# The causal mask of a decay matrix: a minimum on VectorE in place of two TensorE matmuls, and additions moved ahead of a weight split

## The chip, the core and the metric

The kernel runs on one core of a Trainium2 chip. The metric is the device time of one execution in microseconds (us); lower is better. TensorE (PE in the profile) multiplies matrices, VectorE (DVE) and ScalarE (ACT) work elementwise, GpSimd (POOL) helps, and SyncE's queue (SPq) starts the loads. Each engine works through its own instructions in order; engines wait for each other on semaphores.

## What is computed

Two small models run one after the other, each of two layers on 256 tokens of width 1024. The change is in the first model, in its state space mixer ("SSD"), which works on two chunks of 128 tokens, 4 groups and 8 heads in a group:

```python
x = (xh * dt[..., None]).reshape(bsz, nc, SSD_CHUNK, SSD_GROUPS, SSD_HPG, p)
a_cum = jnp.cumsum(a_dt, axis=-1)
causal = jnp.tril(jnp.ones((SSD_CHUNK, SSD_CHUNK), dtype=bool))
decay = jnp.exp(jnp.where(causal, a_cum[..., :, None] - a_cum[..., None, :], -jnp.inf))
cb = jnp.einsum("bclgn,bcsgn->bgcls", cc, bc)
y_diag = jnp.einsum("bgecls,bcsgep->bclgep", cb[:, :, None] * decay, x)
```

`a_cum` only falls along the tokens, since every `dt * a` is negative. For each group, each chunk t and each of the 8 heads the kernel needs a 128 x 128 matrix exp(a_cum[l] - a_cum[s]) for l >= s and zero elsewhere.

## The kernel before

**Weights.** All weights stream from HBM in chunks of 128 x 2048 float32 (1 MB) through a ring of three slots. For precision each chunk is split: ScalarE writes a rounded copy (`split_high`, L964, tile `w_high`), VectorE writes the rest (`split_low`, L1325, tile `w_low`; every `tt` of VectorE is recorded at L1325), and TensorE makes three products of each pair (L524 to L526 for 512 columns, L752 to L754 for 256). ScalarE may split chunk c once TensorE is done with chunk c-3; SyncE may load chunk c+3 once VectorE has split chunk c.

**Slots.** Each engine's program of a layer is one loop over the chunks c, written out. In slot c ScalarE first runs `split_high(l, c)`, VectorE first `split_low(l, c)`, and behind it each runs whatever other work has that slot number; TensorE runs `before(l, c)`, the small matmuls of that slot, and then the products of chunk c. So everything that ScalarE or VectorE does in a slot stands between two splits.

**The SSD work of one group.** Group g starts with weight tile i = 2, 5, 8, 11 (`XT`), and its steps have slots counted from 2i:
- 2i+5: TensorE turns the convolved x of the group (`conv`) into banks 4 and 5. This *turn* waits for `ssd_y` of group g-1, since banks 4 and 5 still hold that group's result. For groups 1 to 3 slot 2i+5 is slot 2i'+11 of the group before (i' = i-3).
- 2i+6 and 2i+8: the *row spread* of chunk t = 0 and 1 (L606 and L608): for each of two banks one matmul of `ident_r` with `never_r` writes -1e30 where l < s and 0 elsewhere, and one matmul adds a_cum[l] of 4 heads, spread over all partitions, on top. GpSimd prepares its operand `decay_rows` (L1293).
- 2i+7 and 2i+9: ScalarE takes 8 exponentials of 128 x 128 from banks 6 and 7 into `ssd_decay` (EM in the code, L1083), with -a_cum[s] as bias; exp(-1e30) is zero.
- 2i+7: VectorE makes y = D x and xdt = dt x from banks 4 and 5 (four instructions). TensorE's state matmul (L614) into bank 6 waits for the exponentials of t = 0; ScalarE copies it out in slot 2i+8 (L1075), and the row spread of t = 1 waits for that copy.
- 2i+8 and 2i+10: VectorE multiplies `ssd_decay` by the masked C B product. TensorE multiplies by xdt in slots 2i+9 and 2i+10 (L633), and by the state in slot 2i+10 (L638).
- 2i+11 and 2i+12: VectorE adds the results into y: one instruction in the first slot, three in the second. The last one signals `ssd_y` for this group; GpSimd's gate (L1287, y times silu(z)) and the next turn wait for it.
- 2i+13: ScalarE squares the gated y (L1089), sums and takes the root; VectorE takes the reciprocal (L1482) and scales. It is the same slot as 2i+7 of the next group, and stands ahead of that group's y and xdt.
- 2i+15: VectorE weights the turned y (two instructions from PSUM), ScalarE rounds it (L1096), VectorE subtracts (two instructions into `b_low`). It is slot 2i+9 of the next group.
- Slots of other work between: a convolution on VectorE (slot 2i+10 for groups 0 to 2, 16 instructions, L1381 and L1384) and rotary embeddings (8 small instructions in slots 2i+7 of group 0 and 2i+9 of the others).

Of the kernel before, what the change touches and what calls it, by code (L numbers as in the profile page):

```python
# [17 lines left out]
F32R = mybir.dt.float32r  # L18
# [4 lines left out]
P = 128  # L23
# [113 lines left out]
def build(nc, stream1, stream2, pars, const1, const2, onehot, relb, final_g, ple_g, w_x, out, rev):  # L137
    ctx = ExitStack()
    with ctx:
# [23 lines left out]
        ident_r = sb("ident_r", [P, P], F32R)  # L163
        never_r = sb("never_r", [P, P], F32R)
# [150 lines left out]
        def signal(name, per):  # L315
            return Signal(sem(name), per)
# [55 lines left out]
        ssd_m = signal("ssd_m", 2 * GROUPS)  # L372
        ssd_y = signal("ssd_y", 2 * GROUPS)
# [148 lines left out]
        def _(pe):  # L522
# [19 lines left out]
            def before(l, c):  # L542
# [37 lines left out]
                for g, i in enumerate(XT):  # L580
                    if c == 2 * i + 5:
                        pe.wait_ge(conv_act.sem, conv_act.at(l, 3 + g))
                        if g == 0:
                            pe.wait_ge(btok_out.sem, btok_out.at(l, 1))
                            pe.wait_ge(cumt_out.sem, cumt_out.at(l, 1))
                        else:
                            pe.wait_ge(ssd_y.sem, ssd_y.at(l, 2 * g))
                        for t in range(T):
                            for j in range(4):
                                last = turn(ps[:, 4 + t, tok(j)], conv[:, j, tok(t)])  # L590
                        last.then_inc(xt_ps.sem, 1)
                    for t, at_c in ((0, 2 * i + 6), (1, 2 * i + 8)):
                        if c == at_c:

                            if t == 1:
                                pe.wait_ge(state_out.sem, state_out.at(l, g + 1))
                            elif g == 0:
                                pe.wait_ge(cb_masked.sem, cb_masked.at(l, 1))
                            else:
                                pe.wait_ge(ssd_y.sem, ssd_y.at(l, 2 * g))  # L600
                                pe.wait_ge(qk_out.sem, qk_out.at(l, g))

                            pe.wait_ge(decay_rows.sem, decay_rows.at(l, g + 1))
                            half_of = (tri_r, later_r)[t][:, P // 2 - 1:P // 2].to_broadcast([P, P])
                            for b in range(2):
                                nc.tensor.matmul(four(ps[:, 6 + b, :]), ident_r[:, :], bc(never_r[:, :].unsqueeze(1), 4, P),  # L606
                                                 start=True, stop=False)
                                last = nc.tensor.matmul(ps[:, 6 + b, :], half_of, DR[:, b * 512:(b + 1) * 512],  # L608
                                                        start=False, stop=True)
                            last.then_inc(row_ps.sem, 1)  # L610
                    if c == 2 * i + 7:
                        pe.wait_ge(xds_ready.sem, xds_ready.at(l, g + 1))
                        pe.wait_ge(ssd_exp.sem, ssd_exp.at(l, 2 * g + 1))
                        nc.tensor.matmul(ps[:, 6, :], btok[:, g, :], xds, start=True, stop=True).then_inc(state_ps.sem, 1)  # L614
# [11 lines left out]
                for g, i in enumerate(XT):  # L626
# [9 lines left out]
                    if c == 2 * i + 10:  # L636
                        pe.wait_ge(ssd_exp.sem, ssd_exp.at(l, 2 * g + 2))
# [315 lines left out]
        def _(act):  # L953
# [36 lines left out]
            with act.Fori(0, L) as l:  # L990
# [17 lines left out]
                for c in range(3, CHUNKS1):  # L1008
# [61 lines left out]
                    for g, i in enumerate(XT):  # L1070
# [5 lines left out]
                        for t, at_c in ((0, 2 * i + 7), (1, 2 * i + 9)):  # L1076
                            if c == at_c:
                                act.wait_ge(row_ps.sem, row_ps.at(l, 2 * g + t + 1))
                                if g:
                                    act.wait_ge(yd_ps.sem, yd_ps.at(l, 2 * (g - 1) + t + 1))  # L1080
                                for e in range(HPG):
                                    a = t * HEADS + g * HPG + e
                                    ins = nc.scalar.activation(EM[t][:, e, :], ps[:, 6 + e // 4, tok(e % 4)], ACT.Exp,  # L1083
# [182 lines left out]
        def _(pool):  # L1266
            pool.wait_ge(late_loaded, 16)
            nc.gpsimd.tensor_copy(ident_r[:, :], ident)
            nc.gpsimd.tensor_scalar(never_r[:, :], later, NEG, None, ALU.mult)
# [51 lines left out]
        def _(dve):  # L1321
# [76 lines left out]
            with dve.Fori(0, L) as l:  # L1398
# [37 lines left out]
                for c in range(3, CHUNKS1):  # L1436
                    split_low(l, c)
# [12 lines left out]
                    for g, i in enumerate(XT):  # L1450
# [5 lines left out]
                        if c == 2 * i + 7:  # L1456
# [8 lines left out]
                            ins.then_inc(xdt_ready.sem, 1)  # L1465
                        for t, at_c in ((0, 2 * i + 8), (1, 2 * i + 10)):
# [3 lines left out]
                        if c == 2 * i + 11:  # L1470
                            dve.wait_ge(yd_ps.sem, yd_ps.at(l, 2 * g + 1))
                            tt(y[:, 0, :], y[:, 0, :], ps[:, 4, :], ALU.add).then_inc(ssd_y.sem, 1)
                        if c == 2 * i + 12:
                            dve.wait_ge(yd_ps.sem, yd_ps.at(l, 2 * g + 2))
                            tt(y[:, 1, :], y[:, 1, :], ps[:, 5, :], ALU.add)
                            dve.wait_ge(off_ps.sem, off_ps.at(l, g + 1))
                            dve.wait_ge(decays.sem, decays.at(l, 1))
                            chain.then(dve, tt(heads(yoff), heads(ps[:, 7, :]), bc(dec_in[:, hs].unsqueeze(2), HPG, HD), ALU.mult))
                            tt(y[:, 1, :], y[:, 1, :], yoff, ALU.add).then_inc(ssd_y.sem, 1)
# [379 lines left out]
```

## Time and profile before

| | us |
|---|---|
| median of 3 runs | 1676.93 (1672.54 to 1677.43) |
| the profiled execution, its device time | 1677.54 |
| its span in the trace | 1675.6 |
| TensorE busy | 1584.4 (95%) |
| VectorE busy | 1022.4 (61%) |
| ScalarE busy | 844.9 (50%) |
| GpSimd busy | 64.3 (4%) |
| mean granted TensorE clock | 0.983 |

The span is that of one execution; 1.9 us of its device time lie around it. Matmuls overlap in the records, so the time that one costs is the distance between two starts, not its recorded duration. The steps of groups 1 and 2 repeat every 43.5 us (turns start at 126.59, 170.08 and 213.54 us), and the SSD work of the two layers lies at about 80 to 260 us and 723 to 903 us.

### The profile page before, as it was taken

The numbers are of one execution on the slowest core, as the hardware profiler recorded it, in microseconds if no ns is written. First come the engines' busy times: TensorE is split into PE (matmuls) and PEld (weight loads), VectorE is DVE, ScalarE is ACT, GpSimd is POOL, SyncE is SP. The second block draws the span as 40 slices with busy tenths as digits, with TensorE's granted clock in tenths as the row PEclk, the third lists the DMA queues.
The fourth block names the chain that finished last, engine by engine and source line by source line (L and its number), as shares of the span: only waits on it lengthen the run. The fifth ranks groups of instructions, "written<-read, shape, count | busy, mean of one in ns | idle before, by whom it ended". The sixth has DMA issues, their size and how long they took to land.

```text
span 1675.6 us, 21488 instructions
## 1 busy us (share of the span) xinstructions
PE 1584.4 (95%) x8006; PEld 1333.9 (80%) x8006; DVE 1022.4 (61%) x1287; ACT 844.9 (50%) x940; POOL 64.3 (4%) x38
## 2 busy tenths in 40 slices
PE   5999999999999997999999999999999799879987
PEld 4988888787778886988888788778888688668876
DVE  5977766545555444777775645565453665666664
ACT  3556666454354433556666444354443555554463
POOL 0001100000000000011100000000000010001000
PEclk9999999999999999999999999999999899999999
DMA  5443444444445553444444434345555453336250
GB/s 198 151 172 135 146 176 152 150 151 151 153 178 179 181 183 140 152 176 151 151 144 159 151 133 155 139 177 181 188 188 187 192 180 108 146 124 226 100 199 33
DMA packets 39666, 265.47 MB, mean 158 GB/s; under 512 B 4343, under 2 KB 5400, under 8 KB 9112
## 3 DMA queue, kind: packets, MB, share of 16 engines
q1 hardware_dynamic: 37800, 260.41, 43.4%
q10 hardware_dynamic: 1776, 3.83, 0.6%
q8 instruction: 60, 0.98, 0.2%
q14 instruction: 30, 0.25, 0.0%
HBM read 262.39 MB, written 1.84 MB: 158 GB/s over the span
## 4 chain that ended last, share of the span: by engine, by line
PE 83%; DVE 5%; issue 5%; ACT 5%; DMA 1%; ACTq 0%; DVEq 0%; SPq 0%
PE ps L524 22%; PE ps L526 21%; PE ps L525 21%; PE ps L529 4%; PE ps L752 3%; PE ps L753 3%; PE ps L754 3%; ACT w_high L964 2%; DVE scratch L1325 2%; PE ps L633 2%; ACT w_high L1154 1%; PE ps L667 1%; DVE w_low L1325 1%; DMA w_raw<-in_stream 1%; DVE h L1325 1%
## 5 line engine op out<-in xcount | busy, mean ns | idle before, releaser
L1325 DVE TENSOR_TENSOR w_low<-w_raw,w_high 128x2048 fp32r<-128x2048 f32 (+2 forms) x252 | 561.0, 2233 | 519.8 <-ACT w_high L964 441.0
L964 ACT ACTIVATE w_high<-w_raw 128x2048 fp32r<-128x2048 f32 (+1 forms) x198 | 372.6, 1884 | 426.4 <-PE ps L526 414.4
L524 PE MATMUL ps<-w_high,u_high 128*128 128x512 f32 x1376 | 553.2, 402 | 10.8 <-DVE w_low L1325 5.8
L526 PE MATMUL ps<-w_high,u_low 128*128 128x512 f32 x1376 | 541.1, 393 | 0.0
L525 PE MATMUL ps<-w_low,u_high 128*128 128x512 f32 x1376 | 540.4, 393 | 0.0
L524 PEld LDWEIGHTS ps<-w_high,u_high 128*128 128x128 f32 x1376 | 261.4, 190 | 67.7 <-issue 7.1
L526 PEld LDWEIGHTS ps<-w_high,u_low 128*128 128x128 f32 x1376 | 261.0, 190 | 56.2
L525 PEld LDWEIGHTS ps<-w_low,u_high 128*128 128x128 f32 x1376 | 261.5, 190 | 53.8 <-issue 1.9
L524 PE MATMUL ps<-w_high,b_high 128*128 128x512 f32 x384 | 151.7, 395 | 1.9 <-issue 1.9
L526 PE MATMUL ps<-w_high,b_low 128*128 128x512 f32 x384 | 149.7, 390 | 0.0
L525 PE MATMUL ps<-w_low,b_high 128*128 128x512 f32 x384 | 149.5, 389 | 0.0
L1154 ACT ACTIVATE w_high<-w_raw 128x2048 fp32r<-128x2048 f32 (+2 forms) x54 | 95.8, 1785 | 96.9 <-PE ps L526 85.2
L529 PE MATMUL ps<-con,scratch 128*128 128x128 f32 x592 | 86.8, 289 | 57.5 <-DVE scratch L1349 29.7
L529 PEld LDWEIGHTS ps<-con,scratch 128*128 128x128 f32 x592 | 73.7, 149 | 72.9 <-DVE scratch L1349 31.2
L752 PE MATMUL ps<-u_high,w_high 128*128 128x256 f32 x384 | 110.2, 287 | 0.0
L753 PE MATMUL ps<-u_low,w_high 128*128 128x256 f32 x384 | 108.7, 283 | 0.0
L754 PE MATMUL ps<-u_high,w_low 128*128 128x256 f32 x384 | 108.7, 283 | 0.0
L524 PEld LDWEIGHTS ps<-w_high,b_high 128*128 128x128 f32 x384 | 72.2, 188 | 16.7 <-issue 2.3
L526 PEld LDWEIGHTS ps<-w_high,b_low 128*128 128x128 f32 x384 | 72.1, 188 | 15.4
L525 PEld LDWEIGHTS ps<-w_low,b_high 128*128 128x128 f32 x384 | 72.2, 188 | 14.1
L752 PEld LDWEIGHTS ps<-u_high,w_high 128*128 128x128 f32 x384 | 73.8, 192 | 0.9 <-issue 0.5
L753 PEld LDWEIGHTS ps<-u_low,w_high 128*128 128x128 f32 x384 | 73.7, 192 | 0.8 <-issue 0.5
(224 smaller groups left out, 1400.9 us busy)
## 6 DMA issues: line engine op xcount, KB each, us to landing
w_raw<-in_stream SPq DMA_DIRECT2D x238, 1024.0 KB, 4.8
w_raw<-in_stream SPq DMA_DIRECT2D x10, 512.0 KB, 3.4
par<-in_pars SPq DMA_DIRECT2D x4, 265.0 KB, 5.0
h<-in_x SPq DMA_DIRECT2D x1, 1024.0 KB, 7.7
ple_gain<-in_ple_g ACTq DMA_DIRECT2D x2, 512.0 KB, 6.1
scratch<-rev ACTq DMA_DIRECT2D x2, 512.0 KB, 6.9
w_raw<-in_stream SPq DMA_DIRECT2D x4, 256.0 KB, 2.5
out<-h SPq DMA_DIRECT2D x2, 512.0 KB, 2.6
```

The source lines that it names most:

```text
L524: nc.tensor.matmul(o, hi, whi, start=start, stop=False, **kw)
L525: nc.tensor.matmul(o, hi, wlo, start=False, stop=False, **kw)
L526: return nc.tensor.matmul(o, lo, whi, start=False, stop=stop, **kw)
L529: return nc.tensor.transpose(o, i, ident)
L633: last = nc.tensor.matmul(ps[:, 4 + t, e * HD:(e + 1) * HD], EM[t][:, e, :], xdt[:, t, e * HD:(e + 1) * HD], start=True, stop=True)
L667: nc.tensor.matmul(ps[:, 4 + g // 2, (g % 2) * S:(g % 2 + 1) * S], qT[:, g, hh, tok(1)], kT[:, hh, :], start=True, stop=True)
L752: nc.tensor.matmul(o, WH[:, slot, w], uH[:, kk, :], start=first, stop=False, skip_group_check=True)
L753: nc.tensor.matmul(o, WH[:, slot, w], uL[:, kk, :], start=False, stop=False, skip_group_check=True)
L754: last = nc.tensor.matmul(o, WL[:, slot, w], uH[:, kk, :], start=False, stop=kk == KD - 1, skip_group_check=True)
L964: nc.scalar.activation(WH[:, c % RING, 0:n], W[:, c % RING, 0:n], ACT.Copy).then_inc(high_ready, 1)
L1154: nc.scalar.activation(WH[:, c % RING, 0:n], W[:, c % RING, 0:n], ACT.Copy).then_inc(high_ready, 1)
L1325: return nc.vector.tensor_tensor(out=o, in0=a, in1=b, op=op)
```

## The change

The two `never_r` matmuls of each row spread are gone, and the spread is a plain matmul. A new VectorE instruction in slots 2i+7 and 2i+9, behind y and xdt, takes min(a_cum[l], a_cum[s]) from banks 6 and 7 into `ssd_decay`; where l < s this is a_cum[s], so that the exponential is 1, and the product with the masked C B makes it zero. ScalarE's exponentials read and write `ssd_decay` in place. Who waited for the exponentials to free banks 6 and 7 now waits for the minimum (`row_clipped`). The additions into y keep their slot numbers but stand ahead of the slot's `split_low`.

```diff
                             for b in range(2):
-                                nc.tensor.matmul(four(ps[:, 6 + b, :]), ident_r[:, :], bc(never_r[:, :].unsqueeze(1), 4, P),
-                                                 start=True, stop=False)
                                 last = nc.tensor.matmul(ps[:, 6 + b, :], half_of, DR[:, b * 512:(b + 1) * 512],
-                                                        start=False, stop=True)
+                                                        start=True, stop=True)
                             last.then_inc(row_ps.sem, 1)
                     if c == 2 * i + 7:
                         pe.wait_ge(xds_ready.sem, xds_ready.at(l, g + 1))
-                        pe.wait_ge(ssd_exp.sem, ssd_exp.at(l, 2 * g + 1))
+                        pe.wait_ge(row_clipped.sem, row_clipped.at(l, 2 * g + 1))
...
                     if c == 2 * i + 10:
-                        pe.wait_ge(ssd_exp.sem, ssd_exp.at(l, 2 * g + 2))
+                        pe.wait_ge(row_clipped.sem, row_clipped.at(l, 2 * g + 2))
...
                             if c == at_c:
-                                act.wait_ge(row_ps.sem, row_ps.at(l, 2 * g + t + 1))
-                                if g:
-                                    act.wait_ge(yd_ps.sem, yd_ps.at(l, 2 * (g - 1) + t + 1))
+                                act.wait_ge(row_clipped.sem, row_clipped.at(l, 2 * g + t + 1))
                                 for e in range(HPG):
                                     a = t * HEADS + g * HPG + e
-                                    ins = nc.scalar.activation(EM[t][:, e, :], ps[:, 6 + e // 4, tok(e % 4)], ACT.Exp,
+                                    ins = nc.scalar.activation(EM[t][:, e, :], EM[t][:, e, :], ACT.Exp,
                                                                bias=nacum[:, a:a + 1])
...
             pool.wait_ge(late_loaded, 16)
-            nc.gpsimd.tensor_copy(ident_r[:, :], ident)
-            nc.gpsimd.tensor_scalar(never_r[:, :], later, NEG, None, ALU.mult)
...
                 for c in range(3, CHUNKS1):
+                    for g, i in enumerate(XT):
+                        if c == 2 * i + 11:
+                            dve.wait_ge(yd_ps.sem, yd_ps.at(l, 2 * g + 1))
+                            tt(Y[g % 2][:, 0, :], Y[g % 2][:, 0, :], ps[:, 4, :], ALU.add).then_inc(ssd_y.sem, 1)
+                        if c == 2 * i + 12:
+                            dve.wait_ge(yd_ps.sem, yd_ps.at(l, 2 * g + 2))
+                            tt(Y[g % 2][:, 1, :], Y[g % 2][:, 1, :], ps[:, 5, :], ALU.add)
...
+                            tt(Y[g % 2][:, 1, :], Y[g % 2][:, 1, :], yoff, ALU.add).then_inc(ssd_y.sem, 1)
                     split_low(l, c)
...
+                        for t, at_c in ((0, 2 * i + 7), (1, 2 * i + 9)):
+                            if c == at_c:
+                                dve.wait_ge(row_ps.sem, row_ps.at(l, 2 * g + t + 1))
+                                if g:
+                                    dve.wait_ge(yd_ps.sem, yd_ps.at(l, 2 * (g - 1) + t + 1))
+                                tt(EM[t], ps[:, 6:8, :].rearrange("p b (e l) -> p (b e) l", e=4),
+                                   bc(acum[:, t * HEADS + g * HPG:t * HEADS + (g + 1) * HPG].unsqueeze(2), HPG, P), ALU.min)\
+                                    .then_inc(row_clipped.sem, 1)
```

VectorE, before, from the end of slot 20 to the scaling in slot 23 (the additions of group 1 in slots 21 and 22; its `ssd_y` is the last `scratch<-scratch` row):

```order
L1384 SCALAR_TENSOR_TENSOR conv<-xpad,par,conv 128x256 x4
L1329 REGISTER_ALU
L1325 TENSOR_TENSOR w_low<-w_raw,w_high 128x2048
L1325 TENSOR_TENSOR scratch<-scratch,ps 128x512
L1329 REGISTER_ALU
L1325 TENSOR_TENSOR w_low<-w_raw,w_high 128x2048
L1325 TENSOR_TENSOR scratch<-scratch,ps 128x512
L1325 TENSOR_TENSOR scratch<-ps,small 128x512
L119 REGISTER_ALU
L1325 TENSOR_TENSOR scratch<-scratch 128x512
L1329 REGISTER_ALU
L1325 TENSOR_TENSOR w_low<-w_raw,w_high 128x2048
```

And the same place of the change, where the file's lines have shifted by 7 (`tt` is L1318):

```order
L1377 SCALAR_TENSOR_TENSOR conv<-xpad,par,conv 128x256 x4
L1318 TENSOR_TENSOR scratch<-scratch,ps 128x512
L1322 REGISTER_ALU
L1318 TENSOR_TENSOR w_low<-w_raw,w_high 128x2048
L1318 TENSOR_TENSOR scratch<-scratch,ps 128x512
L1318 TENSOR_TENSOR scratch<-ps,small 128x512
L119 REGISTER_ALU
L1318 TENSOR_TENSOR scratch<-scratch 128x512
L1322 REGISTER_ALU
L1318 TENSOR_TENSOR w_low<-w_raw,w_high 128x2048
L1322 REGISTER_ALU
L1318 TENSOR_TENSOR w_low<-w_raw,w_high 128x2048
```

One split fewer stands ahead of the last addition, and two splits in a row stand behind it.

VectorE, before, in slots 18 and 19 (the product of t = 0 of group 1, the weighting of group 0, its `b_low`, the rotary embedding):

```order
L1325 TENSOR_TENSOR w_low<-w_raw,w_high 128x2048
L1468 REGISTER_ALU
L1325 TENSOR_TENSOR ssd_decay_54<-ssd_decay_54,scratch 128x1024
L1329 REGISTER_ALU
L1325 TENSOR_TENSOR w_low<-w_raw,w_high 128x2048
L1325 TENSOR_TENSOR scratch<-ps,par 128x512 x2
L1325 TENSOR_TENSOR b_low<-scratch,b_high 128x4x128 x2
L1500 REGISTER_ALU
L1325 TENSOR_TENSOR scratch<-scratch,con 128x128
```

And of the change, from the last xdt instruction of slot 17 on:

```order
L1318 TENSOR_TENSOR xdt<-ps,small 128x512
L1473 REGISTER_ALU
L1318 TENSOR_TENSOR ssd_decay_54<-ps,small 128x1024
L1322 REGISTER_ALU
L1318 TENSOR_TENSOR w_low<-w_raw,w_high 128x2048
L1318 TENSOR_TENSOR ssd_decay_54<-ssd_decay_54,scratch 128x1024
L1322 REGISTER_ALU
L1318 TENSOR_TENSOR w_low<-w_raw,w_high 128x2048
L1318 TENSOR_TENSOR scratch<-ps,par 128x512 x2
L1318 TENSOR_TENSOR b_low<-scratch,b_high 128x4x128 x2
L1473 REGISTER_ALU
L1318 TENSOR_TENSOR ssd_decay_55<-ps,small 128x1024
```

The minimum of t = 0 stands behind xdt, that of t = 1 behind `b_low`.

## Rows read from the trace of the kernel before

**Rows 1.** The page, part 1: busy us, share of the span, instructions.

```profile
PE 1584.4 (95%) x8006; PEld 1333.9 (80%) x8006; DVE 1022.4 (61%) x1287; ACT 844.9 (50%) x940; POOL 64.3 (4%) x38
```

**Rows 2.** Groups by form: line, operation, shapes, count | busy us, mean ns | idle.

```profile
L606 PE MATMUL ps<-never_r,ident_r 128*128 128x512 f32 x32 | 12.5, 391 | 0.0
...
L1325 DVE TENSOR_TENSOR h<-h,ps 128x1024 f32<-128x1024 f32 x14 | 17.1, 1220 | 33.6 <-PE ps L526 28.1 <-DMA h<-in_x 5.5
...
L1231 ACT ACTIVATE block_scores<-block_scores,small 128x128 f32<-128x128 f32 x8 | 3.1, 391 | 1.2 <-DVE small L1688 1.2
```

**Rows 3.** Timeline of TensorE, layer 1, group 1: start, duration, line.

```profile
126.59 1.06 PE L529 MATMUL ps<-con,conv 128*128 128x128 f32 x8
...
148.00 0.39 PE L606 MATMUL ps<-never_r,ident_r 128*128 128x512 f32 x1
148.23 0.39 PE L608 MATMUL ps<-decay_rows,later_r 128*128 128x512 f32 x1
...
148.93 0.39 PE L524 MATMUL ps<-w_high,u_high 128*128 128x512 f32 x1
...
169.58 0.39 PE L526 MATMUL ps<-w_high,u_low 128*128 128x512 f32 x1
170.08 1.06 PE L529 MATMUL ps<-con,conv 128*128 128x128 f32 x8
```

**Rows 4.** Timeline of VectorE, layer 1, group 1 (start, duration, line; in brackets the idle time before).

```profile
135.25 0.68 DVE L1325 TENSOR_TENSOR xdt<-ps,small 128x512 f32<-128x512 f32 x1
...
148.82 2.73 DVE L1325 TENSOR_TENSOR scratch<-scratch,con 128x128 f32<-128x128 f32 x6
...
165.72 2.29 DVE L1325 TENSOR_TENSOR w_low<-w_raw,w_high 128x2048 fp32r<-128x2048 f32 x1
...
169.24 0.69 DVE L1325 TENSOR_TENSOR scratch<-scratch 128x512 f32<-128x512 f32 x1
```

**Rows 5.** Timeline of ScalarE, layer 1, group 1.

```profile
129.49 0.62 ACT L1089 ACTIVATE scratch<-scratch 128x512 f32<-128x512 f32 x1
...
134.98 2.18 ACT L1083 ACTIVATE ssd_decay<-ps,small 128x128 f32<-128x128 f32 x8 [1.25 <-PE ps L608]
136.99 1.96 ACT L964 ACTIVATE w_high<-w_raw 128x2048 fp32r<-128x2048 f32 x1
...
141.58 0.60 ACT L1075 ACTIVATE scratch<-ps 128x512 f32<-128x512 f32 x1 [1.71 <-PE ps L614]
...
149.13 2.18 ACT L1083 ACTIVATE ssd_decay<-ps,small 128x128 f32<-128x128 f32 x8 [0.96 <-PE ps L608]
```

**Rows 6.** Timeline of GpSimd, layer 1.

```profile
71.01 3.91 POOL L1293 TENSOR_TENSOR decay_rows<-scratch,con 128x1024 fp32r<-128x1024 f32 x1 [62.55 <-ACT scratch L1059]
...
105.69 1.90 POOL L1293 TENSOR_TENSOR decay_rows<-scratch,con 128x1024 fp32r<-128x1024 f32 x1 [12.82 <-PE ps L608]
126.61 2.38 POOL L1287 TENSOR_TENSOR scratch<-scratch 128x1024 f32<-128x1024 f32 x1 [19.02 <-DVE scratch L1325]
...
149.18 1.96 POOL L1293 TENSOR_TENSOR decay_rows<-scratch,con 128x1024 fp32r<-128x1024 f32 x1 [12.11 <-PE ps L608]
```

**Rows 7.** Timeline of VectorE beside GpSimd's first row, and six small ones alone.

```profile
68.67 4.49 DVE L1325 TENSOR_TENSOR w_low<-w_raw,w_high 128x2048 fp32r<-128x2048 f32 x2
73.07 2.96 DVE L1381 TENSOR_SCALAR conv<-xpad,par 128x256 f32<-128x256 f32 x4
...
235.46 1.03 DVE L1325 TENSOR_TENSOR scratch<-scratch,con 128x128 f32<-128x128 f32 x6
```

**Rows 8.** Timeline of TensorE: the same place of layer 1 and of layer 2.

```profile
318.28 0.67 PE L667 MATMUL ps<-scratch 128*128 128x256 f32 x2 [1.98 <-DVE b_low L1325]
...
961.49 0.67 PE L667 MATMUL ps<-scratch 128*128 128x256 f32 x2 [1.97 <-DVE b_low L1325]
```

**Rows 9.** Windows of 1 us: PE, PEld, DVE, ACT, POOL busy, granted clock, DMA.

```profile
319.00:320.00 1.00, 1.00 (x8) 0.92 (x7) 1.00 (x1) 0.16 (x1) 0.00 (x0) 1.00 0.08 16
...
963.00:964.00 1.00, 1.00 (x5) 0.91 (x4) 0.79 (x1) 0.00 (x0) 0.00 (x0) 0.50 0.00 0
```

More of the change, by code:

```diff
@@ L162, in build @@
         later_r = nc.alloc_sbuf_tensor_at("later_r", [P, P], F32R, offset=con_at + K_LATER * 4)
-        ident_r = sb("ident_r", [P, P], F32R)
-        never_r = sb("never_r", [P, P], F32R)
         dtw_h = sb("dtw_h", [P, KD * HEADS], F32R)
@@ L372, in build @@
         ssd_m = signal("ssd_m", 2 * GROUPS)
+        row_clipped = signal("row_clipped", 2 * GROUPS)
         ssd_y = signal("ssd_y", 2 * GROUPS)
@@ L1436, in _ @@
                 for c in range(3, CHUNKS1):
+                    for g, i in enumerate(XT):
[5 more added lines that the diff above has]
+                            tt(Y[g % 2][:, 1, :], Y[g % 2][:, 1, :], ps[:, 5, :], ALU.add)
+                            dve.wait_ge(off_ps.sem, off_ps.at(l, g + 1))
+                            dve.wait_ge(decays.sem, decays.at(l, 1))
+                            chain.then(dve, tt(yoff.rearrange("p (e d) -> p e d", e=HPG), ps[:, 7, :].rearrange("p (e d) -> p e d", e=HPG),
+                                               bc(dec_in[:, g * HPG:(g + 1) * HPG].unsqueeze(2), HPG, HD), ALU.mult))
+                            tt(Y[g % 2][:, 1, :], Y[g % 2][:, 1, :], yoff, ALU.add).then_inc(ssd_y.sem, 1)
                     split_low(l, c)
@@ L1469, in _ @@
                                 tt(EM[t], EM[t], bc(cbm[:, t, g, :].unsqueeze(1), HPG, P), ALU.mult).then_inc(ssd_m.sem, 1)
[L1470 to L1479, printed above, removed]
                         if c == 2 * i + 13:
```

## The prediction, as it was put on record

> **What bounds the kernel now.** First the page: TensorE is busy 1584.4 of 1675.6 us and every other engine at most 61% [rows 1], so what is taken from TensorE counts unless it waits for something instead. Then TensorE's timeline over groups 1 and 2 of the SSD work. The turn of group 1 starts at 126.59, that of group 2 at 170.08, 43.49 us later [rows 3]. The last matmul ahead of the second starts at 169.58, 0.50 ahead, where the usual distance of such matmuls is 0.23 (148.00 to 148.23) [rows 3]. So TensorE waits 0.27 us there and works 43.22 us in a period. Last, VectorE's timeline for what it waits for: the last addition into y starts at 169.24 and takes 0.69, so `ssd_y` comes at 169.93, and the turn follows 0.15 later [rows 3, 4]. The stage is thus near two limits at once: TensorE's own work, and the chain ScalarE, VectorE, GpSimd that leads from one `ssd_y` to the next. The change shortens the first and rearranges the second, so both have to be worked out.
>
> **TensorE's part.** There are 32 masking matmuls, with no idle time ahead of them [rows 2]. Four starts (two masking, two spreading) fill 148.00 to 148.93 [rows 3], so each masking one costs 0.23, a spread gets 0.46 shorter, and a period of two spreads needs 43.22 - 0.93 = 42.29 us. Over 32 that is 7.4 us. With the 0.27 wait of three turns in each of two layers (1.6 us) the most that can be won is 9.0 us. The recorded 391 ns would make it 12.5, but those records overlap. The two GpSimd instructions that go at the start take under 1 us, at about 7 us, when TensorE's first work is still 9 us off: nothing.
>
> **The new instruction.** The minimum reads 1024 columns of PSUM and writes SBUF. Its nearest row is the addition h + PSUM of the same size, 1.22 us [rows 2]; the range is 1.13 (the distance to the next instruction in such rows) to 1.3. The exponential can start 0.04 after it. Before, it started 0.44 after the last spreading matmul's start (148.69, and 149.13 in [rows 5]). In place exponentials read SBUF: 391 ns recorded in the nearest row [rows 2], against 384 from PSUM, so their distance stays 2.01 for eight (134.98 to 136.99) [rows 5].
>
> **Group 0.** Nothing of an earlier group stands ahead of its minimum of t = 1, so that starts with the spread's signal. The exponentials, and all behind them up to `ssd_y`, come 1.26 later; the split that now stands behind the additions takes 2.20 out (its row at 165.72 recorded 2.29, the next starts 2.20 on) [rows 4]. Net 0.94 earlier against TensorE's spread, of which TensorE needs 0.27. The first turn moves from 126.59 to 125.41: 0.93 and 0.27 gained, rounded. `ssd_y` is at 124.60.
>
> **Group 1, from one `ssd_y` to the next.** (a) The gate. The split of slot 16 starts at about 124.50, 0.1 before the last addition ends, and GpSimd's gate would start 0.16 after that end. What happens to such a pair is in the trace. GpSimd's 128x1024 product that started at 71.01, just after the second of two splits (68.67, 4.49 for two), took 3.91 instead of the 1.90 of its twin at 105.69, and its end at 74.92 is 1.8 after the split's; VectorE's next four instructions took 2.96, and it was the turn of VectorE to stand [rows 6, 7]. So I let the gate (2.38 alone [rows 6]) begin when the split ends, near 126.75, and end at 129.13. ScalarE squares at 129.17, where before it did at 129.49 [rows 5] against a turn 1.18 later: a delay of 0.86. (b) From there to the last xdt instruction at 135.25, and 0.60 on, is 6.36 [rows 4, 5]: the minimum of t = 0 starts at 135.53. (c) Exponentials at 136.79 (134.98 before), the split by ScalarE at 138.80 (136.99), state copy at 141.58 as before, since it had waited 1.71 [rows 5]; most of this delay is absorbed. (d) VectorE's split of slot 18 at 140.80, the product until 144.13, the split of slot 19 until 146.34, weighting, and `b_low` ready to start at 147.72. (e) The minimum of t = 1 stands behind `b_low`. GpSimd's rows for the next group start when the spread is done, at 147.08. Before they met the rotary instructions at 149.18, six of which took 2.73 instead of 1.03 while GpSimd took 1.96 [rows 4, 6, 7]; that cost nothing, as VectorE had idle time behind them. Now they hold back `b_low` until 148.98, and the minimum starts at 150.20. Behind this wait stand the exponentials and both engines' splits of slot 20. (f) Exponentials at 151.46 (149.13 before). From there it was 20.80 to `ssd_y` [rows 4, 5]; less the 2.20 of the moved split it is 18.60: 170.06, and the turn at 170.21. TensorE would be ready at 125.41 + 42.29 = 167.70 and waits 2.5 us. Before, the turn was at 170.08: the 1.2 us of group 0 are given back, and 0.1 more.
>
> The rule in the Trainium skill, SBUF — State Buffer, Who interferes with whom, says the same of (a) and (e) and speaks against this change: a VectorE instruction with both inputs in SBUF and a GpSimd instruction that reads SBUF exclude each other for the whole instruction, whichever starts first. The rows at 71.01 and 73.07 agree. By that rule the sum is the one worked out here; if nothing collided it would be rival A's. It also says that with one SBUF input there is no such contention, which would leave the minimum free of it; no row here shows that.
>
> **Group 2.** Turn at 170.21, `ssd_y` at 170.06. The gate waits until 172.25 and ends near 174.6, so the squares come 4.43 after the turn instead of 2.90. With the same steps: minimum of t = 0 at 181.0, product until 189.6, split until 191.8, `b_low` at 193.8 (GpSimd holds it 0.6), minimum 195.0, exponentials 196.3, `ssd_y` 214.9, turn 215.0. Before: 213.54; 1.5 lost.
>
> **Group 3** has no convolution behind it and no turn that waits for it at once. The work from its turn to TensorE's next meeting with `ssd_y` (slot 33, at 256.15 before) was 42.61; without the masks 41.68, so 256.7. The state matmul needs the minimum by 228.2 and has it at 227.1; the product of t = 1 is there at 248.0, needed at 248.6. A layer ends 0.6 later, two layers 1.1.
>
> **The clock.** After a wait of 1.98 us at 318.28 TensorE's granted clock stayed at 1.00 (2.4 GHz); after its twin of 1.97 us at 961.49 it went to 0.50 (1.2 GHz) for about 3.6 us [rows 8, 9], in which half the work is done: 1.8 us lost. The change makes four such waits. Behind turn 2 the chain has 2.5 us to hide it; behind turn 3 it shows. At one in two that is 1.8 us for two layers, at most 3.6.
>
> **The sum** against the profiled execution's 1677.54: + 1.1 + 1.8 makes 1680.4 (a span of 1678.5 and the 1.9 around it). The median of the runs is 0.6 lower, and without any fall of the clock it would be 1678.0; I take 1679 between the two.
>
> **Rivals.** (A) *GpSimd does not matter*: neither the gate nor the rows collide with VectorE as I say. Then the minimum of t = 1 starts 0.45 late in groups 1 and 2 only. TensorE waits 0.4 at turn 2 and 3 (turns at 168.1 and 210.8), a layer wins 3.7, and the kernel takes 1669.6. For it: the gate's recorded start may hide who comes first, by 0.26 us. Against it: the rows at 71.01. (B) *The second split goes first*, the slower one. Two splits stand in a row behind `ssd_y`. If VectorE keeps the operands over both, the gate begins 2.2 later. In group 1 the second split isn't ready (ScalarE's is done at 127.3), but in groups 2 and 3 it is, as TensorE's wait lets ScalarE run ahead. Then turn 3 comes 2.2 later, group 3's product misses TensorE by 1.7, a layer loses 4.5, and the kernel takes 1686. Against it: at 73.07 GpSimd came in between two VectorE instructions. It decides from 0.95 us more in each of the four periods on, which would take the sum from +1.1 to +5. (C) *The minimum doesn't matter and TensorE's gain is whole*, 1668: against it stand (e) and (f), whatever GpSimd does.
>
> **Chances.** A measurement of this kernel can tell about 0.3%, 5 us. My forecast 0.58, with times from 1675 to 1682, all within 0.3%. Rival A 0.17, C 0.05, both faster by more. B 0.10, and 0.10 for other delays in the chain that all come four times: slower by more. Range 1669 to 1685: from A to just under B, which leaves out C and B.
>
> **What the profile would show.** Two spreading matmuls 0.23 apart in each spread. The minimum at about 1.2 us. The gate at 4.4 instead of 2.4 us in all four groups. `b_low` of slots 19 and 25 near 2 to 2.5 us instead of 1.3. TensorE's turn at 125.4, then 2.5 us waits for VectorE ahead of the next two. A gate of 2.4 us, or turns 42.3 us apart, would prove me wrong towards A or C; a gate over 6 us towards B.

## The result, and the profile after

| | us |
|---|---|
| before, median of 11 runs | 1676.06 (1671.24 to 1678.13) |
| the change, median of 11 runs | 1680.59 (1674.71 to 1683.55) |
| ratio | 1.0032 [1.0021, 1.0043] |
| the profiled execution of the change | 1683.21, a span of 1681.4 |

The change makes the kernel 0.32% slower. One execution of `rows_again` below, of 4690 us, is disturbed and left out of its ratio; the profile fell on it, so no trace of that run is read. The page of the changed kernel, part 1 (before: [rows 1]):

```profile
PE 1583.6 (94%) x7974; PEld 1334.2 (79%) x7974; DVE 1045.5 (62%) x1303; ACT 847.6 (50%) x940; POOL 79.3 (5%) x36
```

TensorE has 32 matmuls fewer, and GpSimd, which got no new work, is busy 15.0 us longer: its records now hold waiting. TensorE's timeline shows the turns (before: [rows 3]):

```profile
125.16 1.04 PE L528 MATMUL ps<-con,conv 128*128 128x128 f32 x8
...
146.10 0.63 PE L605 MATMUL ps<-decay_rows,later_r 128*128 128x512 f32 x2
146.57 0.40 PE L523 MATMUL ps<-w_high,u_high 128*128 128x512 f32 x1
...
170.03 1.76 PE L528 MATMUL ps<-con,conv 128*128 128x128 f32 x8 [2.42 <-DVE scratch L1318]
...
192.65 0.63 PE L605 MATMUL ps<-decay_rows,later_r 128*128 128x512 f32 x2
...
216.44 1.06 PE L528 MATMUL ps<-con,conv 128*128 128x128 f32 x8 [2.28 <-DVE scratch L1318]
...
258.19 1.04 PE L528 MATMUL ps<-con,scratch 128*128 128x128 f32 x8
```

The spread fills 0.47 (146.10 to 146.57), where it filled 0.93. Turns 2 and 3 come 44.87 and 46.41 us behind the ones ahead of them (before 43.49 and 43.46), each behind a wait for VectorE. The spread of t = 1 starts 20.94 behind turn 1 (146.10) and 22.62 behind turn 2 (192.65). The last row is TensorE's meeting with `ssd_y` in slot 33, 41.75 behind turn 3.

GpSimd and VectorE, groups 1 and 2, between turns (before: [rows 4, 6]):

```profile
124.75 4.29 POOL L1280 TENSOR_TENSOR scratch<-scratch 128x1024 f32<-128x1024 f32 x1 [18.34 <-DVE scratch L1318]
135.61 1.05 POOL L1272 TENSOR_TENSOR scratch<-xdt,small 128x512 f32<-128x512 f32 x1 [6.57 <-DVE xdt L1318]
146.81 1.90 POOL L1286 TENSOR_TENSOR decay_rows<-scratch,con 128x1024 fp32r<-128x1024 f32 x1 [10.15 <-PE ps L605]
...
193.36 2.37 POOL L1286 TENSOR_TENSOR decay_rows<-scratch,con 128x1024 fp32r<-128x1024 f32 x1 [11.34 <-PE ps L605]
```

```profile
124.50 2.28 DVE L1318 TENSOR_TENSOR w_low<-w_raw,w_high 128x2048 fp32r<-128x2048 f32 x1
127.31 3.88 DVE L1318 TENSOR_TENSOR w_low<-w_raw,w_high 128x2048 fp32r<-128x2048 f32 x1 [0.53 <-ACT w_high L961]
...
135.45 1.21 DVE L1318 TENSOR_TENSOR ssd_decay<-ps,small 128x1024 f32<-128x1024 f32 x1
...
147.91 1.94 DVE L1318 TENSOR_TENSOR b_low<-scratch,b_high 128x512 fp32r<-128x512 f32 x2
149.78 1.21 DVE L1318 TENSOR_TENSOR ssd_decay<-ps,small 128x1024 f32<-128x1024 f32 x1
...
193.28 3.00 DVE L1318 TENSOR_TENSOR b_low<-scratch,b_high 128x512 fp32r<-128x512 f32 x2
196.19 1.21 DVE L1318 TENSOR_TENSOR ssd_decay<-ps,small 128x1024 f32<-128x1024 f32 x1
```

The gate takes 4.29 instead of 2.38: recorded from 124.75, it gets its operands when the split of VectorE ends (126.78), and the next split, of 127.31, then stands until the gate ends (129.04; it takes 3.88, and ends 2.15 behind the gate). The third row of GpSimd is the one that counts. From 146.81 to 148.71 it makes the rows of the next group, and both `b_low` instructions, ready at 147.91, stand behind it. They take 1.07 together from there, and the minimum of t = 1 starts at 149.78. In group 2 one `b_low` gets ahead of the rows: these end at 195.73, the other `b_low` takes 0.46 behind them, and the minimum starts at 196.19. The minimum itself has one input in SBUF; beside GpSimd's row of 135.61 it takes the same 1.21, and that row the 1.05 that it takes in every group.

ScalarE's exponentials, now in place (before: [rows 5]):

```profile
136.70 2.45 ACT L1078 ACTIVATE ssd_decay<-ssd_decay,small 128x128 f32<-128x128 f32 x8 [3.37 <-DVE ssd_decay L1318]
139.05 1.90 ACT L961 ACTIVATE w_high<-w_raw 128x2048 fp32r<-128x2048 f32 x1
```

From the first of the eight to the split behind them it is 2.35, where it was 2.01. Last, windows of 1 us behind turn 2 (PE, PEld, DVE, ACT, POOL busy, granted clock, DMA):

```profile
169.00:170.00 1.00, 0.00 (x0) 0.00 (x1) 0.97 (x3) 0.56 (x1) 0.00 (x0) 1.00 0.82 156
170.00:171.00 1.00, 0.97 (x6) 1.00 (x7) 1.00 (x1) 0.00 (x0) 0.96 (x1) 0.62 0.91 385
171.00:172.00 1.00, 1.00 (x6) 1.00 (x5) 1.00 (x1) 0.00 (x0) 1.00 (x1) 0.50 0.97 410
172.00:173.00 1.00, 1.00 (x6) 1.00 (x6) 1.00 (x2) 0.00 (x0) 1.00 (x1) 0.50 0.30 115
173.00:174.00 1.00, 1.00 (x6) 0.87 (x5) 1.00 (x1) 0.47 (x1) 1.00 (x1) 0.67 1.01 131
```

After the wait TensorE's clock falls to 0.50 (1.2 GHz). The shares missing in these windows add up to 1.7 us of work lost, 3.4 us at half speed. It does so behind turn 2 of both layers here, and behind turn 3 of neither.

### The profile page after: what moved, and what is told of

Its sections match the earlier page's. It is cut to its first block, busy times and chain, and to the rows that moved or that the text cites. A ratio compares the mean times of both kernels' runs of the same rounds, so it can differ in the third digit from the quotient of the medians.

```text
span 1681.4 us, 21440 instructions
## 1 busy us (share of the span) xinstructions
PE 1583.6 (94%) x7974; PEld 1334.2 (79%) x7974; DVE 1045.5 (62%) x1303; ACT 847.6 (50%) x940; POOL 79.3 (5%) x36
## 4 chain that ended last, share of the span: by engine, by line
PE 71%; DVE 12%; ACT 8%; issue 8%; DMA 1%; POOL 1%; DVEq 0%; ACTq 0%; SPq 0%; POOLq 0%
PE ps L523 19%; PE ps L525 19%; PE ps L524 19%; PE ps L528 4%; ACT w_high L961 3%; DVE scratch L1318 3%; DVE w_low L1318 2%; PE ps L749 2%; PE ps L750 2%; PE ps L751 2%; DVE conv L1377 1%; DVE ssd_decay L1318 1%; ACT ssd_decay L1078 1%; PE ps L664 1%; ACT w_high L1149 1%
## 5 line engine op out<-in xcount | busy, mean ns | idle before, releaser
L1318 DVE TENSOR_TENSOR w_low<-w_raw,w_high 128x2048 fp32r<-128x2048 f32 (+2 forms) x252 | 570.3, 2270 | 501.7 <-ACT w_high L961 422.1
```

What stands on the lines that cost most here:

```text
L1318: return nc.vector.tensor_tensor(out=o, in0=a, in1=b, op=op)
```

## The experiments

Theory from these rows: from turn 1 to turn 2 there are two chains, which meet at the minimum of t = 1. One goes through gate, squares, minimum of t = 0, exponentials and splits on VectorE and ScalarE. The other goes through TensorE's own work to the spread, GpSimd's rows, `b_low`. From the minimum of t = 1 to the next turn is fixed work. The rivals were that the gate's longer time costs, that either half of the change costs by itself, that the minimum costs nothing, and later that with one delay gone another takes its place. The kernels were measured in three sets, each on another chip and beside the kernel before: at 1677.10 us (median of 19 runs), 1677.13 (21) and 1675.24 (26). Ratios are to the kernel before of the same set. Times of the stage are read from turn to turn in the one trace of each run; *lost work* is what the granted clock takes away, added up over windows of 1 us. Diffs are against the changed kernel; all versions compute everything.

### The two halves alone

`mask_only` (first set, as are `move_only`, `gate_vector` and `blow_behind`) has the minimum, with the additions behind their slots' splits as before. `move_only` has the masking matmuls and exponentials of before, with the additions ahead.

The first, against the changed kernel:

```diff
                 for c in range(3, CHUNKS1):
-                    for g, i in enumerate(XT):
-                        if c == 2 * i + 11:
-                            dve.wait_ge(yd_ps.sem, yd_ps.at(l, 2 * g + 1))
-                            tt(Y[g % 2][:, 0, :], Y[g % 2][:, 0, :], ps[:, 4, :], ALU.add).then_inc(ssd_y.sem, 1)
...
                     split_low(l, c)
...
+                        if c == 2 * i + 11:
+                            dve.wait_ge(yd_ps.sem, yd_ps.at(l, 2 * g + 1))
...
```

The second is the kernel before with the same lines moved the other way.

> The minimum and the in-place exponentials alone; the additions into y stand behind their slot's split as before. Theory (the chain from one ssd_y to the next sets the period, and the moved additions take one split of 2.2 us out of it): without the move the first turn comes about 0.7 us later than before, turns 2 and 3 follow at about 47.3 us instead of 43.5, TensorE waits about 5 us ahead of each, and the kernel is about 15 us slower than before (1690 to 1695). Rival (the moved additions are what costs, through the collision of GpSimd's gate with the split behind them): the minimum alone costs nothing and the kernel is as fast as before or faster, down to 1669. In this kernel the gate should again take 2.4 us.

> The additions ahead of the split alone; the masking matmuls and the exponentials from PSUM stay. Theory: ssd_y comes 2.2 us earlier, TensorE's wait of 0.27 us at three turns in two layers goes, which is 1.6 us in all: 1674.5, no measurable change. The gate collides with the split (4.3 us instead of 2.4), but it starts 2 us earlier than TensorE needs, so that this costs nothing. Rival (the gate's collision is the cost of the change): slower than before by 2 to 5 us.

Measured: `mask_only` 1691.23 us (1685.38 to 1695.69), ratio 1.0087 [1.0065, 1.011]. `move_only` 1672.58 (1667.55 to 1676.97), ratio 0.9974 [0.9964, 0.9985]. VectorE of `mask_only` at the minimum of t = 1 of group 1, and TensorE's next turn:

```profile
148.62 2.99 DVE L1318 TENSOR_TENSOR b_low<-scratch,b_high 128x512 fp32r<-128x512 f32 x2
151.53 1.22 DVE L1318 TENSOR_TENSOR ssd_decay<-ps,small 128x1024 f32<-128x1024 f32 x1
```

```profile
174.00 1.94 PE L528 MATMUL ps<-con,conv 128*128 128x128 f32 x8 [4.63 <-DVE scratch L1318]
```

From that minimum to the turn it is 22.47, in the changed kernel 20.25 (149.78 to 170.03). The 2.2 between them is the split that the move takes out. Turns are 47.1 us apart in three of the four periods, 48.55 in the last of layer 2. The gates took 2.4, as expected, only in five of the eight groups; behind each wait of 4.6 us, with the next split ready, they took 4.3. The masking by a minimum alone thus costs 14 us of the median; the move earns most of it back, but only because the minimum has made that chain the bound. Without the minimum the move is worth 4.5 us of the median, more than expected, although all its gates take 4.3: the rival, by which the gate's collision is the cost, fails here. The turns of `move_only` are 43.19 apart, 0.3 less than before, so TensorE's own waits explain less than half of it (0.9 us a layer). Its trace has TensorE at the low clock for 28.3 us of lost work over the whole execution, that of before for 30.0: one fall of the clock less is the likely rest, not shown.

### The gate on VectorE

`gate_vector` gives y times silu(z) to VectorE, behind `ssd_y` and ahead of the split. GpSimd doesn't gate any more.

```diff
                             tt(Y[g % 2][:, 1, :], Y[g % 2][:, 1, :], yoff, ALU.add).then_inc(ssd_y.sem, 1)
+                            dve.wait_ge(ssd_y.sem, ssd_y.at(l, 2 * g + 2))
+                            dve.wait_ge(tile_out.sem, tile_out.at(l, ZT[g] + 1))
+                            tt(Y[g % 2], Y[g % 2], ev[0], ALU.mult).then_inc(y_gated.sem, 1)
...
-                    gate(g)
```

> The change, with the gate on VectorE right behind ssd_y instead of on GpSimd, so that gate and split can't collide. Theory (the minimum of t = 1 waits for b_low, which waits for GpSimd's rows of the next group, and that hides what the late gate costs): the turn of group 2 does not move (period 44.9), that of group 3 comes 1.4 to 3.2 us earlier, and the kernel is 3 to 6 us faster than the change: 1674 to 1678. Rival (the gate's collision is the main cost): periods near 43 us, 8 us or more faster than the change: below 1672.

Measured: 1681.28 us (1677.85 to 1683.26), ratio 1.0032 [1.0019, 1.0045]; nothing won. The minimum of t = 0 came at 134.45, 1.0 earlier than in the change, and that of t = 1 didn't move:

```profile
146.92 2.94 DVE L1312 TENSOR_TENSOR b_low<-scratch,b_high 128x512 fp32r<-128x512 f32 x2
149.78 1.22 DVE L1312 TENSOR_TENSOR ssd_decay<-ps,small 128x1024 f32<-128x1024 f32 x1
```

`b_low` started 1.0 earlier and took 1.0 longer. GpSimd's rows start with TensorE's spread, at 146.81 as before, and hold it until 148.71. So the gate's collision, real as it is, isn't what costs. The expectation was right that turn 2 stays (44.88) and wrong that turn 3 gains: that period is 46.43 here, 46.41 in the change. In that period even the minimum of t = 0 comes no earlier (180.81 in both): behind turn 2 the clock fell, ScalarE's copy of what TensorE turned starts at 173.53 in both, and the squares stand behind that copy, not behind the gate.

### `b_low` behind the minimum

`blow_behind` moves the two `b_low` instructions behind the minimum of t = 1 in the same slot. They belong to group g and the minimum to group g+1; a second loop over the groups puts them behind it (the lines without a mark are unchanged, and now stand in that loop). It was measured in two of the sets.

```diff
                                    bc(par[:, C_SN + 4 * g:C_SN + 4 * g + 4].unsqueeze(2), 4, P), ALU.mult).then_inc(y_weighted.sem, 1)
+                    for g, i in enumerate(XT):
+                        if c == 2 * i + 15:
                             for t in range(T):
                                 dve.wait_ge(y_high.sem, y_high.at(l, 2 * g + t + 1))
...
```

> The change, with the two b_low instructions of slot 2i+15 behind the minimum of t = 1 of the next group. GpSimd's rows then run while VectorE reads PSUM. Theory: minimum of t = 1 at 22.6 us behind the turn in group 1 and 23.1 in group 2 (24.6 and 26.2 in the change), periods of 42.8 and 43.3 us, a layer ends 2.9 us earlier than before: 1670, 10 us faster than the change. Rival (the gate): 1678 or more, since the gate still takes 4.3 us.

Measured: 1669.35 us (1668.38 to 1670.62), ratio 0.9958 [0.9945, 0.9971], and once more:

> The kernel with b_low behind the minimum of t = 1 once more, beside the three others on one chip: 1669 to 1670, ratio 0.996.

1669.45 (1666.51 to 1670.81), ratio 0.9953 [0.9941, 0.9966]. VectorE and TensorE:

```profile
147.18 1.22 DVE L1318 TENSOR_TENSOR ssd_decay<-ps,small 128x1024 f32<-128x1024 f32 x1
148.31 1.28 DVE L1318 TENSOR_TENSOR b_low<-scratch,b_high 128x512 fp32r<-128x512 f32 x2
```

```profile
167.44 1.06 PE L528 MATMUL ps<-con,conv 128*128 128x128 f32 x8 [0.40 <-DVE scratch L1318]
...
210.73 1.06 PE L528 MATMUL ps<-con,conv 128*128 128x128 f32 x8 [0.81 <-DVE scratch L1318]
```

The minimum reads PSUM and a small tile and doesn't stand behind the rows. It comes 22.59 behind the turn instead of 24.62, the turn 20.26 behind it as ever, and TensorE waits 0.4 and 0.8 instead of 2.4. From group 0's turn to slot 33 a layer takes 168.4 us, where the change takes 173.5 and the kernel before 171.2. One place in VectorE's program turns 0.3% slower into 0.4% faster.

### The rows later

`rows_late` leaves VectorE's order alone and lets GpSimd make the rows behind the minimum of t = 1.

```diff
-                        pool.wait_ge(row_ps.sem, row_ps.at(l, 2 * g))
+                        pool.wait_ge(row_clipped.sem, row_clipped.at(l, 2 * g))
```

> The change, with one wait altered: GpSimd makes the next group's decay_rows once VectorE's minimum of t = 1 is done, not once TensorE's spread is. It then runs beside the rotary embedding, as before the change. My theory (the rows push b_low and the minimum of t = 1 back): b_low takes 1.3 us in groups 1 and 2, the minimum of t = 1 starts 0.7 to 1.7 us earlier, the turns of layer 1 lie 44.2 and about 44.7 us apart instead of 44.87 and 46.41, a layer is 2.3 us shorter, and the kernel takes about 1676, as before the change. Rival (the rows only fill a gap that something else would fill, as the gate's collision proved to): turns and time as with the change, 1680 to 1681.

> Late rows alone, once more. The trace of the first run showed each layer some 2.4 us shorter, but its ten times fell in two heaps, 1674.5 to 1679.4 at granted clocks of 0.981 to 0.984 and 1680.9 to 1683.1 at 0.979 to 0.981, with the median in the upper one. If that was chance, 1676 to 1678 now; if late rows really cost something outside the stage, 1680 again.

VectorE, and TensorE's turns:

```profile
147.84 1.29 DVE L1318 TENSOR_TENSOR b_low<-scratch,b_high 128x512 fp32r<-128x512 f32 x2
149.05 1.22 DVE L1318 TENSOR_TENSOR ssd_decay<-ps,small 128x1024 f32<-128x1024 f32 x1
```

```profile
125.07 1.03 PE L528 MATMUL ps<-con,conv 128*128 128x128 f32 x8
...
169.31 1.06 PE L528 MATMUL ps<-con,conv 128*128 128x128 f32 x8 [1.82 <-DVE scratch L1318]
...
213.97 1.06 PE L528 MATMUL ps<-con,conv 128*128 128x128 f32 x8 [2.19 <-DVE scratch L1318]
```

The stage did what was expected: `b_low` at 1.29, turns 44.24 and 44.66 apart. The time did not: 1680.16 us (1674.52 to 1683.06), ratio 1.0018 [1.0004, 1.0032], and the second time 1680.29, ratio 1.0029 [1.0016, 1.0041]. In the one trace the clock fell behind turn 3 of layer 2, where no slack follows, and not behind turn 2:

```profile
860.00:861.00 1.00, 1.00 (x6) 1.00 (x5) 1.00 (x2) 0.00 (x0) 1.00 (x1) 0.50 0.36 139
861.00:862.00 1.00, 1.00 (x3) 0.78 (x3) 1.00 (x1) 0.97 (x1) 1.00 (x1) 0.50 0.59 82
```

Over the whole trace two falls' worth more was lost than before (33.3 us against 30.0), one of them this one, and the seven executions of both sets that took over 1680 us of span had a mean clock of 0.979 where before has 0.983. That fits the missing 3 to 4 us; why late rows should draw more falls stays open.

### Both chains shortened

`gate_rows` joins the gate on VectorE with the late rows; `both` joins the gate on VectorE with `b_low` behind the minimum. Their diffs are those above.

> The change, with the gate on VectorE and GpSimd's rows behind the minimum of t = 1 (two earlier edits together). Theory: two chains run side by side from a turn to the minimum of t = 1, and the later one counts. One goes over TensorE's spread and GpSimd's rows (spread done, 1.90 for the rows, 1.07 for b_low, then the minimum: 24.62 behind the turn), the other over gate, squares, minimum of t = 0, exponentials and splits (23.98 behind the turn in the run with late rows). Moving the gate alone shortened the second and won nothing; moving the rows alone took the first away and won 0.63 in group 1. With both gone the gate's 1.0 us must show: turns 43.3 us apart in group 1 and 43.3 to 43.7 in group 2, against 44.24 and 44.66 with late rows alone. The kernel then takes 1672 to 1674. Rival (the gate is off the chain altogether, the splits set the pace): turns 44.2 and 44.7, the time as with late rows.

> The change, with b_low behind the minimum of t = 1 and the gate on VectorE (the two edits of the earlier runs together). Theory: with b_low behind the minimum alone the turns were 42.85 and 43.29 us apart, 0.5 and 1.0 above TensorE's own work, and what is left is the gate's 2 us ahead of the minimum of t = 0, which now has nothing behind it to be absorbed in. Then TensorE waits nowhere, turns are 42.3 us apart, a layer is 4.5 us shorter than the change's, and the kernel takes 1667 to 1668. Rival (the minimum of t = 0 is absorbed by the split behind it also here, as it was when the gate alone was moved): the same as b_low behind the minimum alone, 1669 to 1671.

`gate_rows`: 1669.95 us (1666.61 to 1673.42), ratio 0.9976 [0.9964, 0.9989]; turns at 123.97, 167.19 and 210.38:

```profile
146.93 1.22 DVE L1312 TENSOR_TENSOR ssd_decay<-ps,small 128x1024 f32<-128x1024 f32 x1
```

```profile
167.19 1.06 PE L528 MATMUL ps<-con,conv 128*128 128x128 f32 x8 [0.77 <-DVE scratch L1312]
...
210.38 1.06 PE L528 MATMUL ps<-con,conv 128*128 128x128 f32 x8 [0.72 <-DVE scratch L1312]
```

The periods are 43.22 and 43.19 (expected 43.3, and 43.3 to 43.7). The gate's microsecond, worth nothing alone, is worth 1.0 and 1.5 once the rows are out of the way. `both`: 1667.08 (1665.02 to 1670.13), ratio 0.9942 [0.9929, 0.9955]. Its turns at 125.53, 167.80 and 210.10 are 42.27 and 42.30 apart, TensorE's own work without any wait. A layer takes 166.9, 1.6 less than in `blow_behind`. It beats both kernels and has the lowest median; its interval and those of `blow_behind` overlap, so only the traces of the stage tell these two apart.

### The minimum back into PSUM

`min_psum` writes the minimum where it read it, and the exponentials read PSUM.

```diff
-                                    ins = nc.scalar.activation(EM[t][:, e, :], EM[t][:, e, :], ACT.Exp,
+                                    ins = nc.scalar.activation(EM[t][:, e, :], ps[:, 6 + e // 4, tok(e % 4)], ACT.Exp,
...
-                                tt(EM[t], ps[:, 6:8, :].rearrange("p b (e l) -> p (b e) l", e=4),
+                                tt(ps[:, 6:8, :].rearrange("p b (e l) -> p (b e) l", e=4), ps[:, 6:8, :].rearrange("p b (e l) -> p (b e) l", e=4),
...
-                        pe.wait_ge(row_clipped.sem, row_clipped.at(l, 2 * g + 1))
+                        pe.wait_ge(ssd_exp.sem, ssd_exp.at(l, 2 * g + 1))
```

> The change, with the minimum written back into PSUM, from where the exponentials read, as before the change; TensorE waits for the exponentials again before it writes into these banks. The values are the same. Theory (eight exponentials of 128 x 128 take 2.36 us when they read SBUF and 2.01 when they read PSUM): the distance from the first exponential to the split behind them is 2.01 again, turns 2 and 3 come about 0.35 us earlier each, and the kernel takes 0.7 to 1.4 us less than the change's, some 1679. Rival (the 0.35 is the in-place use or the write's end, not the source): the distance stays 2.36 and so does the time.

Measured: 1677.35 us (1675.4 to 1681.16), ratio 1.0009 [0.9998, 1.0019]. ScalarE, VectorE and TensorE:

```profile
136.25 2.17 ACT L1078 ACTIVATE ssd_decay<-ps,small 128x128 f32<-128x128 f32 x8 [3.38 <-DVE ps L1318]
138.26 1.96 ACT L961 ACTIVATE w_high<-w_raw 128x2048 fp32r<-128x2048 f32 x1
```

```profile
147.18 2.64 DVE L1318 TENSOR_TENSOR b_low<-scratch,b_high 128x512 fp32r<-128x512 f32 x2
149.74 1.22 DVE L1318 TENSOR_TENSOR ps<-ps,small 128x1024 f32<-128x1024 f32 x1
```

```profile
169.72 1.07 PE L528 MATMUL ps<-con,conv 128*128 128x128 f32 x8 [2.15 <-DVE scratch L1318]
183.92 1.12 PE L611 MATMUL ps<-scratch 128*128 128x512 f32 x2 [0.55 <-ACT ssd_decay L1078]
...
215.16 1.06 PE L528 MATMUL ps<-con,conv 128*128 128x128 f32 x8 [2.15 <-DVE scratch L1318]
```

The distance is 2.01 again. These exponentials read PSUM, and they also no longer read and write one tile; which of the two saves the 0.35 isn't separated. From the minimum of t = 1 to the turn it is 19.98 instead of 20.25. Group 1 gains only 0.12 all the same (44.75), as the rows start 0.14 later (21.79 behind the turn). Group 2 takes 45.44: the state matmul waits for the exponentials (its start is 0.83 behind the last product instead of 0.12), the spread and the rows come that much later (192.21, 22.49 behind the turn), and the minimum with them, at 195.18, again 2.97 behind the rows' start. Behind the turns of its layer 1 the clock did not fall, and in layer 2 only behind turn 3. From group 0's turn to slot 33 the layers take 173.60 and 174.09, the change's 173.55 and 173.47. So the 3 us by which the median is below the change's aren't won in this stage: its trace has 28.0 us of lost work, those of the change 38.1 and 33.7.

### The change once more

> The change as it is, beside the two others on one chip: 1680 to 1681, turns 2 and 3 at 44.87 and 46.4 us behind the ones ahead of them where the clock falls behind turn 2, and 45.3 to 45.7 for the second where it does not.

1680.23 us (1678.47 to 1683.45), ratio 1.0033 [1.0021, 1.0044]; turns 44.88 and 46.39 apart. The clock fell behind turn 2 and behind turn 3, in both layers, so what was expected without a fall behind turn 2 was not seen. Group 3 took 43.37 instead of 41.75 (slot 33 at 259.99):

```profile
170.23 1.94 PE L528 MATMUL ps<-con,conv 128*128 128x128 f32 x8 [2.42 <-DVE scratch L1318]
216.62 1.06 PE L528 MATMUL ps<-con,conv 128*128 128x128 f32 x8 [2.42 <-DVE scratch L1318]
...
259.99 1.04 PE L528 MATMUL ps<-con,scratch 128*128 128x128 f32 x8
```

## Why the prediction was right, and where not

The kernel was forecast at 1679 us, at most 0.3% from before; it takes 1680.59, a ratio of 1.0032, just outside that 0.3% and inside the range. Sign and range were right; the loss itself was put at half its size, 2.1 us above the median before where 4.5 was measured. The lost gain went where the prediction said, into a wait of TensorE ahead of two turns in each layer.

**TensorE's part.** Right: spreads of 0.47, and 42.27 to 42.30 a period where nothing is waited for (`both`), against 42.29.

**The new instruction.** 1.21 as forecast. Wrong was that the exponentials keep their 2.01 in place; 2.35 was measured, and 2.01 again in `min_psum`, where they read PSUM and write another tile. Only the eight of t = 1 are on the path, 0.3 in each period.

**Group 0.** Right: turn at 125.16 in a trace that starts 0.27 earlier (125.43 against 125.41).

**Group 1.** (a) The gate: ending 129.04 + 0.27 against 129.13 forecast, squares at 129.07 + 0.27 against 129.17. Right in size, and with the row of 124.75 the trace agrees with the rule of the Trainium skill, SBUF — State Buffer, Who interferes with whom; its other half, no contention with one SBUF input, is now shown too, by the minimum of 135.45. But steps (a) to (d) carry nothing: `gate_vector` took (a) away and the period stayed. The prediction's own figures have it: `b_low` ready at 147.72, the rows until 148.98, so that its minimum at 150.20 comes from (e) alone, from the rows behind TensorE's spread. It didn't draw from this that (a) adds nothing, and told the two paths as one chain of delays. (e) Right: minimum at 149.78 + 0.27 against 150.20. (f) 20.25 to the turn against 20.01, the exponentials again. Turn 2 at 170.30 by the clock of before, against 170.21. Of the 2.4 us of wait in that period, the rows' collision makes 0.6 by itself (`rows_late`), and it and the gate's make 1.65 together (`gate_rows`). The order of `b_low` and the minimum makes 2.0 (`blow_behind`), and `both` takes away all of it.

**Group 2.** The step that failed: period 44.8 forecast, 46.41 measured. `b_low` was to be held for 0.6, by rows 21.67 behind the turn; it was held for 1.7 (3.00 instead of 1.29), by rows at 23.33. Rows at 21.65, as in group 1, would end at 23.55 and let the minimum start 1.07 later, at 24.62 as there; with 20.25 to the turn that is 44.87 again. This is an estimate, as no trace of the change lacks a fall of the clock in this group. `rows_late` does, and its spread comes 20.96 behind turn 2 (190.27) and its `b_low` 23.19, which fits.

**The clock.** That is its cause. The prediction let a fall behind turn 2 vanish in the chain's 2.5 us of slack, and counted only falls behind turn 3, at 1.8 us. A fall behind turn 2 delays the spread, and with it rows, `b_low` and minimum, by 1.7 (22.62 behind the turn instead of 20.94), since that path has no slack. By the estimate above it costs 1.5 a layer (46.41 - 44.87), and it came in all four layers traced of this kernel. The falls behind turn 3 came in two of the four, as assumed, and cost 1.6 in either layer of the second trace (43.37 - 41.75 in layer 1).

**Group 3.** 41.75 against 41.68.

**The sum.** Layer 1 ends 2.31 later (258.19 + 0.27 - 256.15), where the forecast had 0.55; 1.6 of the difference is group 2, the rest the exponentials and roundings. Layer 2 takes 2.23 more from group 0's turn on. That is 4.54 for the two against + 1.1 and + 1.8 for the clock, 2.9 in all. The span grew by 5.8; the other 1.3 lies outside the stage. The trace of the change has 38.1 us of lost work against 30.0 before, and 3.4 of it in the stage, so falls elsewhere can make the 1.3; that isn't shown.

**The rivals.** A (GpSimd does not matter) and C (the minimum does not matter) fell with a gate of 4.29 and turns 44.87 apart; it took `both` to get C's time. B (the second split goes first) fell too: gates of 4.27 to 4.31 in all groups, also where ScalarE was far ahead.

## What to carry to other kernels

Before you add up delays from one wait to the next, draw the paths that run side by side and take the later at each meeting: a collision that costs 1 us on one path was worth nothing until the other was shortened, and then all of it. An instruction that others wait for goes ahead of one that can be held up by another engine; exchanging two on VectorE was worth 11 us here. Where work is moved to an engine whose chain is as long as the bound, count what stands ahead of it there, and look for the path that begins in the bounding engine itself: a lower clock makes that one longer too.

## What the runs showed of the hardware

- When GpSimd's and VectorE's two-input SBUF instructions meet, GpSimd gets in between two VectorE instructions that have no wait between them (rows in between the two `b_low`, 3.00 for the pair instead of 1.29).
- Eight ScalarE activations of 128 x 128 take 2.35 us to the next instruction when they read and write one SBUF tile, and 2.01 when they read PSUM and write SBUF, though their recorded durations, 388 and 384 ns, hardly differ.
- TensorE's clock falls to 0.50 for 3.4 us at a time, 1.7 us of work each. In the traces of these kernels it fell behind each of the ten waits of 2.42 or 2.43 us ahead of a turn, and behind two of the eight of 2.15 to 2.28. The two traces of the change differ by 4.4 us of lost work. Its executions follow the granted clock, from 1674.71 us at 0.983 to 1683.45 at 0.978, so falls are probably most of the spread of its times.
